# Seven products with features and rests side by side, output tiles kept in PSUM, and w_out's rests on GpSimd

## What is computed

```python
def swiglu(x, w_in, w_out):
    gate, up = jnp.split(x @ w_in, 2, axis=-1)
    return (jax.nn.silu(gate) * up) @ w_out
h = layer_norm(DN_ALPHA * h + 0.5 * swiglu(h, ffn_w_in[i, 0], ffn_w_out[i, 0]), ln_g[i, 0], ln_b[i, 0])
```

## Time and profile before

| | |
|---|---|
| median of three runs | 2694.2 us |
| profiled execution | 2693.18 us, span 2691.6 us |
| mean granted clock of TensorE | 0.997 |
| TensorE busy | 2646.5 us, 98%, 15,901 matmuls |
| VectorE busy | 1937.9 us, 72% |
| ScalarE busy | 1123.7 us, 42% |
| GpSimd busy | 577.0 us, 21% |
| memory | 99 GB/s over the span |

### The profile page before, as it was taken

The page is one execution under the profiler, slowest core; times in us unless marked ns, Lnnn a source line. Parts: engine busy times, 40 slices in busy tenths (PEclk is TensorE's granted clock), DMA queues, the critical chain, the costliest instruction groups (busy, mean ns, idle before and its releaser), DMA issues.

```text
span 2691.6 us, 38695 instructions
## 1 busy us (share of the span) xinstructions
PE 2646.5 (98%) x15901; PEld 2303.0 (86%) x15901; DVE 1937.9 (72%) x2651; ACT 1123.7 (42%) x1624; POOL 577.0 (21%) x366
## 2 busy tenths in 40 slices
PE   9899999999999999999999999999999999999998
PEld 6787877678899997888999988999988888889997
DVE  7888634656888865448888778888655745788876
ACT  4444555543433445353434444434432332444343
POOL 2211000101444400001544214444000000044440
PEclk9999999999999999999999999999999999999999
DMA  9543222212333332222333323333323223233331
GB/s 303 157 150 107 63 63 63 79 52 78 122 94 106 99 110 66 92 63 73 116 97 121 108 72 121 95 107 98 110 83 110 78 72 110 78 108 97 94 110 63
DMA packets 297891, 268.34 MB, mean 100 GB/s; under 512 B 11047, under 2 KB 265265, under 8 KB 297586
## 3 DMA queue, kind: packets, MB, share of 16 engines
q1 hardware_dynamic: 294050, 256.99, 30.9%
q0 software_dynamic: 2368, 6.64, 0.7%
q10 hardware_dynamic: 1296, 2.23, 0.3%
HBM read 263.72 MB, written 2.10 MB: 99 GB/s over the span
## 4 chain that ended last, share of the span: by engine, by line
PE 81%; DVE 12%; ACT 3%; issue 3%; POOL 1%; DMA 0%; DVEq 0%; POOLq 0%; ACTq 0%
PE psum L368 14%; PE psum L370 14%; PE psum L369 14%; PE psum L448 7%; PE psum L449 7%; PE psum L450 7%; PE psum L424 2%; PE psum L425 2%; PE psum L426 2%; PE psum L3040 1%; DVE w_lo L353 1%; DVE w_lo L1130 1%; PE psum L3053 1%; PE psum L1621 1%; PE psum L2608 1%
## 5 line engine op out<-in xcount | busy, mean ns | idle before, releaser
L368 PE MATMUL psum<-h_hi,w_hi 128*128 128x256 f32 (+1 forms) x2224 | 720.0, 324 | 12.8 <-DVE consts L1153 4.2
L370 PE MATMUL psum<-h_hi,w_lo 128*128 128x256 f32 (+1 forms) x2224 | 701.8, 316 | 0.0
L369 PE MATMUL psum<-h_lo,w_hi 128*128 128x256 f32 (+1 forms) x2224 | 701.4, 315 | 0.0
L368 PEld LDWEIGHTS psum<-h_hi,w_hi 128*128 128x128 f32 x2224 | 425.5, 191 | 47.7 <-issue 9.7
L369 PEld LDWEIGHTS psum<-h_lo,w_hi 128*128 128x128 f32 x2224 | 425.5, 191 | 28.4 <-issue 4.8
L370 PEld LDWEIGHTS psum<-h_hi,w_lo 128*128 128x128 f32 x2224 | 425.1, 191 | 27.0
L1076 POOL TENSOR_TENSOR val<-w_raw 128x512 f32<-128x512 f32 x72 | 100.4, 1395 | 963.5 <-DMA w_raw<-in_ffn_w_in 567.9
L353 DVE TENSOR_TENSOR w_lo<-w_raw,w_hi 128x2048 fp32r<-128x2048 f32 x98 | 223.1, 2287 | 83.4 <-ACT w_hi L348 77.3
L544 DVE SCALAR_TENSOR_TENSOR acc<-psum,acc 128x512 f32<-128x512 f32 x374 | 242.2, 679 | 36.0 <-PE psum L450 35.4
L368 PE MATMUL psum<-t_hiffn,w_hi 128*128 128x256 f32 x864 | 244.9, 283 | 0.4
L369 PE MATMUL psum<-t_loffn,w_hi 128*128 128x256 f32 x864 | 244.5, 283 | 0.0
(11 more groups left out here) (460 smaller groups left out, 5603.0 us busy)
## 6 DMA issues: line engine op xcount, KB each, us to landing
w_raw<-in_ffn_w_in SPq DMA_DIRECT2D x176, 512.0 KB, 5.0
w_raw<-in_ffn_w_out SPq DMA_DIRECT2D x88, 512.0 KB, 6.2
w_raw<-in_ret_w_in SPq DMA_DIRECT2D x48, 512.0 KB, 4.6
ada_raw<-in_ada_w SPq DMA_DIRECT2D x32, 512.0 KB, 4.4
w_raw<-in_odd_w_in SPq DMA_DIRECT2D x32, 512.0 KB, 4.8
w_raw<-in_even_w_in SPq DMA_DIRECT2D x24, 512.0 KB, 6.1
w_raw<-in_gla_w_in SPq DMA_DIRECT2D x24, 512.0 KB, 4.8
ada_first<-in_ada_w SPq DMA_DIRECT2D x32, 256.0 KB, 6.2
```

What stands on the lines that cost most here:

```text
L368: k.nc.tensor.matmul(out, ws, xs, start=first, stop=False)
L369: k.nc.tensor.matmul(out, ws, xl, start=False, stop=False)
L370: return k.nc.tensor.matmul(out, wl, xs, start=False, stop=last)
```

## The change

- The rounded features and their rests get neighbouring places in one tile (`k.h`, `k.t`). A group of three 256-column matmuls in the seven products becomes one of 512 columns (rounded weights by rounded features and rests, into the two halves of a bank) and one of 256 columns (`beside`). It concerns rounds 2 to 10 of the four stages.
- Each product then has two halves in its bank, and VectorE adds both (`add_product`, and the new lines of `vector_mid`). The second addition takes the first one's result and waits for it. Product 1 of the next half waits for f_u where it waited for f_p1.
- Of the output tiles of rounds 0 to 7 the four that are made last stay in their PSUM banks; the next round begins with the same tiles and accumulates on them (`kept`, `onto_kept`, `out_order`). VectorE adds only the other four to `acc`.
- The rests of w_out for rounds 2 to 8 are made by GpSimd (`gpsimd_rest`, one subtraction of 128x2048), in its queue between the sums of "a" and those of "b", instead of by VectorE's L353. TensorE and SP wait for GpSimd's event there (`rest_done`).

```diff
+def kept(r):
+    return r < ROUNDS - 3
+def out_order(n):
+    stage, what, r = PIECES[n]
+    return (4, 5, 6, 7, 0, 1, 2, 3) if stage[:3] == "ffn" and what == "o" and r < ROUNDS - 2 and r % 2 else tuple(range(8))
+def onto_kept(n, j):
+    stage, what, r = PIECES[n]
+    return stage[:3] == "ffn" and what == "o" and 0 < r < ROUNDS - 2 and kept(r - 1) and j in out_order(n)[:4]
...
+def pool_rest(n):
+    stage, what, r = PIECES[n]
+    return stage[:3] == "ffn" and what == "o" and SEVEN <= r < ROUNDS - 2
+def rest_done(n):
+    return ("pool_w" if pool_rest(n) else "w_lo", n)
+def gpsimd_rest(k, n):
+    k.nc.gpsimd.wait_ge(*k.at("w_hi", n))
+    k.nc.gpsimd.tensor_tensor(k.lo(n), k.w_raw[:, buffer(n), :], k.hi(n).bitcast(F32), SUB).then_inc(*k.up("pool_w", n))
 def sync_piece(k, n):
     if n in (SLOTS, SLOTS + 1):
         k.nc.sync.wait_ge(*k.at("used", n - SLOTS))
     elif n > SLOTS:
-        k.nc.sync.wait_ge(*k.at("w_lo", n - SLOTS))
+        k.nc.sync.wait_ge(*k.at(*rest_done(n - SLOTS)))
...
+def beside(k, bank, ws, wl, x, first, last):
+    k.nc.tensor.matmul(bank.rearrange("p (a n) -> p a n", a=2), ws, x, start=first, stop=False)
+    return k.nc.tensor.matmul(bank[:, 0:256], wl, x[:, 0, :], start=False, stop=last)
...
-    onto = seeded(n, j)
+    onto = seeded(n, j) or onto_kept(n, j)
...
-    pe.wait_ge(*k.at("w_lo", n))
+    pe.wait_ge(*k.at(*rest_done(n)))
     pe.wait_ge(*k.at(*ready[0]))
-    for j in range(4):
-        pe.wait_ge(*k.at(*free[j]))
+    tiles = out_order(n)
+    for j in tiles[:4]:
+        if not onto_kept(n, j):
+            pe.wait_ge(*k.at(*free[j % 4]))
         out_part(k, n, j, order[0], True, False, hi, lo)
     pe.wait_ge(*k.at(*ready[1]))
-    for j in range(8):
-        if j >= 4:
-            pe.wait_ge(*k.at("acc", (n, j - 4)))
+    for j in tiles:
+        if j not in tiles[:4]:
+            pe.wait_ge(*k.at("acc", (n, j ^ 4)))
             out_part(k, n, j, order[0], True, False, hi, lo)
         ins = out_part(k, n, j, order[1], False, True, hi, lo)
-        ins.then_inc(*(k.up("out", (n, j)) if j < 7 else k.up("used", n)))
+        ins.then_inc(*k.up(*out_done(n, j)))
...
-    return ("out", (n, j)) if j < 7 else ("used", n)
+    return ("out", (n, j)) if j != out_order(n)[-1] else ("used", n)
...
-            event = ("f_p1", "f_c11", "f_c12", "f_c21")[x]
+            event = ("f_u", "f_c11", "f_c12", "f_c21")[x]
...
-        (wh, wl), (xh, xl) = w_block(k, n, a), h_block(k, stage, b)
+        (wh, wl), both = w_block(k, n, a), h_beside(k, stage, b)
         for kk in range(4):
             w = slice(kk * P, (kk + 1) * P)
-            ins = three(k, k.bank[bank][:, 0:256], wh[:, w], wl[:, w], xh[:, kk, :], xl[:, kk, :],
-                        kk == 0, kk == 3)
+            ins = beside(k, k.bank[bank][:], wh[:, w], wl[:, w], both[:, :, kk, :], kk == 0, kk == 3)
...
+def add_product(k, b, out, onto):
+    ve = k.nc.vector
+    ve.tensor_tensor(out, onto, k.bank[b][:, HALF[0]], ADD).then_inc(*k.dve.up())
+    ve.wait_ge(*k.dve.at())
+    return ve.tensor_tensor(out, out, k.bank[b][:, HALF[1]], ADD)
 def vector_mid(k, stage, r, s, x):
     ve, key = k.nc.vector, (stage, r, s)
     u, c22, e, p1 = k.f_c[stage][:, 0, :], k.f_c[stage][:, 1, :], k.f_h[:, s, HALF[1]], k.f_h[:, s, HALF[0]]
-    ve.wait_ge(*k.at("f_p", key + (x + 1,)))
     if x == 0:
         ve.wait_ge(*k.at("f_p1", key))
-        ve.tensor_tensor(u, p1, k.bank[1][:, 0:256], ADD).then_inc(*k.up("f_u", key))
+        ve.tensor_tensor(p1, p1, k.bank[0][:, HALF[1]], ADD).then_inc(*k.dve.up())
+        ve.wait_ge(*k.at("f_p", key + (1,)))
+        ve.wait_ge(*k.dve.at())
+        add_product(k, 1, u, p1).then_inc(*k.up("f_u", key))
     elif x == 1:
+        ve.wait_ge(*k.at("f_p", key + (2,)))
         ve.wait_ge(*k.at("f_u", key))
-        ve.tensor_tensor(e, u, k.bank[2][:, 0:256], ADD).then_inc(*k.up("f_e", key))
+        add_product(k, 2, e, u).then_inc(*k.up("f_e", key))
     else:
+        ve.wait_ge(*k.at("f_p", key + (3,)))
         ve.wait_ge(*k.at("f_e", key))
-        ve.tensor_tensor(c22, e, k.bank[3][:, 0:256], ADD)
-        ve.tensor_tensor(u, u, k.bank[3][:, 0:256], ADD).then_inc(*k.up("f_g", key))
+        ve.tensor_tensor(c22, e, k.bank[3][:, HALF[0]], ADD)
+        ve.tensor_tensor(u, u, k.bank[3][:, HALF[0]], ADD).then_inc(*k.dve.up())
+        ve.wait_ge(*k.dve.at())
+        ve.tensor_tensor(c22, c22, k.bank[3][:, HALF[1]], ADD)
+        ve.tensor_tensor(u, u, k.bank[3][:, HALF[1]], ADD).then_inc(*k.up("f_g", key))
 def vector_c11(k, stage, r, s):
     ve, key, p1 = k.nc.vector, (stage, r, s), k.f_h[:, s, HALF[0]]
     ve.wait_ge(*k.at("f_p", key + (4,)))
-    ve.tensor_tensor(p1, p1, k.bank[1][:, 0:256], ADD).then_inc(*k.up("f_c11", key))
+    add_product(k, 1, p1, p1).then_inc(*k.up("f_c11", key))
 def vector_c12(k, stage, r, s):
     ve, key, e = k.nc.vector, (stage, r, s), k.f_h[:, s, HALF[1]]
     ve.wait_ge(*k.at("f_p", key + (5,)))
-    ve.tensor_tensor(e, e, k.bank[2][:, 0:256], ADD).then_inc(*k.up("f_c12", key))
+    add_product(k, 2, e, e).then_inc(*k.up("f_c12", key))
 def vector_products(k, stage, r, s):
     ve, key, c = k.nc.vector, (stage, r, s), k.f_c[stage]
     ve.wait_ge(*k.at("used", AT[stage, "ab"[s], r]))
     ve.wait_ge(*k.at("f_g", key))
-    ve.tensor_tensor(c[:, 0, :], c[:, 0, :], k.bank[3][:, 0:256], ADD).then_inc(*k.up("f_c21", key))
+    add_product(k, 3, c[:, 0, :], c[:, 0, :]).then_inc(*k.up("f_c21", key))
...
-        vector_piece(k, AT[stage, "o", r - 1])
+        if not pool_rest(AT[stage, "o", r - 1]):
+            vector_piece(k, AT[stage, "o", r - 1])
...
-            vector_outs_ffn(k, stage, r - 1, range(4, 6))
+            if not kept(r - 1):
+                vector_outs_ffn(k, stage, r - 1, range(4, 6))
             vector_unit_s(k, n, 1)
-            vector_outs_ffn(k, stage, r - 1, range(6, 8))
+            if not kept(r - 1):
+                vector_outs_ffn(k, stage, r - 1, range(6, 8))
...
 def vector_outs_ffn(k, stage, r, outs):
+    n = AT[stage, "o", r]
     for j in outs:
-        vector_out(k, AT[stage, "o", r], j, r == 0)
+        vector_out(k, n, out_order(n)[j], r < 2 and j < 4)
...
             gpsimd_sums(k, stage, r, s)
+            if s == 0 and r >= SEVEN + 2:
+                gpsimd_rest(k, AT[stage, "o", r - 2])
...
-    k.h_hi, k.h_lo = sb("h_hi", [P, KD, T], F32R), sb("h_lo", [P, KD, T], F32R)
+    k.h = sb("h", [P, 2, KD, T], F32R)
+    k.h_hi, k.h_lo = k.h[:, 0, :, :], k.h[:, 1, :, :]
...
-            k.t_hi[stage], k.t_lo[stage] = (sb(n + stage, [P, 3, 4, 256], F32R, c2) for n in ("t_hi", "t_lo"))
+            k.t[stage] = sb("t" + stage, [P, 2, 3, 4, 256], F32R, c2)
+            k.t_hi[stage], k.t_lo[stage] = k.t[stage][:, 0, :, :, :], k.t[stage][:, 1, :, :, :]
...
```

More of the change, by code:

```diff
@@ L929, in h_block, with h_beside @@
     return k.h_hi[:, 4 * half:4 * half + 4, HALF[c]], k.h_lo[:, 4 * half:4 * half + 4, HALF[c]]
+def h_beside(k, stage, x):
+    if x in T_BLOCK:
+        return k.t[stage][:, :, T_BLOCK[x], :, :]
+    half, c = H_BLOCK["B12" if x == "T1" else x]
+    return k.h[:, :, 4 * half:4 * half + 4, HALF[c]]
 def w_blocks(k, n, unit, count):
@@ L1337, in vector_seventh @@
     vector_unit_a22(k, n)
-    vector_outs_ffn(k, stage, r - 1, range(4, 8))
     vector_unit_s(k, n, 0)
@@ L1375, in vector_ffn @@
     vector_t_rest(k, stage, "T1")
-    vector_outs_ffn(k, stage, 0, range(4, 8))
     vector_seventh(k, stage)
@@ L3863, in tiles @@
     k.lng, k.lnb = sb("lng", [P, D]), sb("lnb", [P, D])
-    k.f_oh_hi, k.f_oh_lo, k.w4_hi, k.w4_lo, k.t_hi, k.t_lo, k.f_c = {}, {}, {}, {}, {}, {}, {}
+    k.f_oh_hi, k.f_oh_lo, k.w4_hi, k.w4_lo, k.t, k.t_hi, k.t_lo, k.f_c = {}, {}, {}, {}, {}, {}, {}, {}
     k.f_h = k.const("reset128", 0, 2 * T).rearrange("p (a n) -> p a n", n=T)
```

## The result

The changed kernel takes 2857.1 us (median of 4 runs, 2855.1 to 2858.4) against 2694.6 for the kernel before (2692.4 to 2696.4): 1.0603 times as long, 95% interval 1.059 to 1.0616, or 162.6 us more. The profiled execution took 2855.9, its span 2854.5.

What follows compares the result with a forecast made beforehand. The changed stage was taken as bound by TensorE, VectorE's queue close behind. Stalls of 2.0, 0.9 and 1.2 less 0.7 gained, 3.4 us a round x 28 = 95, plus 22 for rounds 2 and 10: +117, 2810 us; range 2728 to 2882.

Steps and rivals of the forecast that it cites:

- rival A: GpSimd's subtraction gets in ahead of L1140 (now L1188); TensorE stalls 3.2 us there, 5.7 a round, 2875 us; chance 0.16.
- order of forecast: In the "a" half, L1140 (now L1188) runs to 8.7 us, then GpSimd's subtraction from 8.6 to 13.2.
- the walk: VectorE's queue followed in written order through a middle round (3 to 9): 3.4 us more a round, 95 in all.
- the stalls: TensorE waits of 2.0 us for f_u and 0.9 for f_g in the "b" half, 1.2 at the output's fifth tile.
- TensorE's gain: One 512- and one 256-column matmul replace three of 256: 12.6 ns saved per group, 0 to 25.4 us, upper taken.
- VectorE's load: Seven adds of a half become fifteen, 7.8 us more a round; less removed work, net +3 on 25.3: fits as a sum.
- the block: VectorE instructions with both inputs in SBUF wait out GpSimd's 4.59 us subtraction; the "a" pair, ready at 11.35, waits until 13.2.
- The kept tiles give TensorE nothing: TensorE did not wait for evacuations before; the tiles' worth is only 2.4 us in VectorE's queue.
- Rounds 2 and 10: Rounds outside the walk: round 2 costs between 2 and 7 us, 4 taken; round 10 +1.6; 22 over four stages.
- rival B: GpSimd's subtraction falls into gaps of VectorE's two-input work: 1.4 us a round, +61, 2754 us; chance 0.20.
- C: VectorE keeps up, f_u of the "b" half being the place; only TensorE's term stands, 2668 us; 0.03 for it and stalls cancelling.
- Rival D: The 512-column matmul saves nothing: forecast with 25 us more, 2835; forecast and this together 0.47.

Runs made afterwards that it cites:

- kept alone: The kernel before with only the kept output tiles: no 512-column matmuls, w_out's rests on VectorE; 2698.7 us, ratio 1.0017.
- no second adds: The changed kernel without VectorE's additions of the second bank halves and with w_out's rests on VectorE; 2684.0 us, 0.996 times the kernel before.
- rests on VectorE: The changed kernel with w_out's rests made by VectorE again, nothing on GpSimd but its sums; 2796.8 us, 1.0375 times the kernel before.
- waits: The changed kernel with one more wait on GpSimd, so its subtraction starts only after VectorE's L1188; 2810.6 us, 1.0428 times the kernel before.

## Why the prediction was right and wrong

The time lay in the range and on the forecast side, 47 us above the forecast; the mechanism was rival A's (2875, given 0.16), 18 us above what was measured. The 162.6 us, split by the runs, each difference with one part changed:

```
kept tiles                        (kept alone - before)            +4.2
512-column matmuls                (no second adds - kept alone)   -14.7
second-half adds                  (rests on VectorE - no adds)   +112.8
subtraction on GpSimd, order of forecast  (waits - on VectorE)    +13.8
the same ahead of L1188           (changed - waits)               +46.6
```

- **The step that failed** is in the walk: "It ends near 7.5; L1140 waits for that, runs to 8.7". `gpsimd_sums` started at 1.73, not near 1.9, took 5.3 us, at 1.30 to 1.32 an instruction, and ended at 7.04; I had carried over 5.6 from a "b" piece, beside which VectorE's pair ran (803.00). With L1188 due at 7.3, as forecast (875.52 is 7.29), the subtraction was first. Two events "within 0.3 us" can't be put in order from sums of such rows. That deserved near even chances, not 0.47 against 0.16; a start 0.5 us later gave the forecast's order, in round 8 of ffn11.
- **Given the order, the walk holds.** The run with the wait is 2810.6 against the forecast's 2810. That it comes so close is partly luck: the stalls came out 0.4 us a round shorter than forecast and TensorE's gain 0.3 smaller, and the two cancel. Its stalls are 1.49, 0.51 and 0.82 as shown; a shown wait starts at a modelled end, and each costs 0.27 more than that between starts (0.16 of the last matmul's overlap and 0.1 of a longer first one), so 1.8, 0.8 and 1.1 against 2.0, 0.9 and 1.2. For the changed kernel the same count gives 4.61 + 4 x 0.27 - 0.38 = 5.3 a round, the 5.3 measured; rival A had 5.7.
- **VectorE's load** was the main term, and it was right that it fits as a sum and not where TensorE waits: 30.77 us busy in 36.37, some 4.2 of them L1188 held in the block. That is 85%, where the forecast named near 90% as its sign. Dependent adds are 0.44 to 0.46 apart inside `add_product` (871.24 to 871.70) and 0.51 to 0.54 across its events, where I took 0.51 for all.
- **TensorE's gain** was mis-sized: 6.8 ns a group, 13.7 us in all, not 12.6 and 25.4. Neither end of 0 to 12.6 was it; the middle would have been the better guess for an operand that no row showed. The Trainium skill ("TensorE: Matmul & The Clock Gate", Back-to-back issue gap) would have made it 5 us, an estimate; the measured 14 lies between.
- **The block** is as told: the trace agrees with the Trainium skill ("SBUF - State Buffer", Who interferes with whom) in the rows shown, 5.40 us at L1188, 2.84 and 4.81 for the pair and for one of its two, and 0.42 for adds with an operand in PSUM.
- **"The kept tiles give TensorE nothing"** was right in steady rounds, and missed that four evacuations less in round 2 move two-input work into GpSimd's way: +4.
- **Rounds 2 and 10** were right: round 2 cost 3.75 us a stage where I took 4, and all outside rounds 2 to 9 5.4 us, 1.35 a stage, where I took 1.6 for round 10. The steps in them were not separated by a run.
- **Round 3** is not the middle round of the walk: its L1188 goes first, and it cost 4.1 us, less than the 5.3 of rounds 4 to 9.
- **The range's lower end**, 2728, is 26 us under rival B, where the bounds given for round 2 make 8. It played no part.
- Rivals B and C are out: in none of the 28 rounds were L1188 and the pair of "a" both free of the block, and VectorE did not keep up even without GpSimd's part (2796.8). Rival D was partly so, by half the gain.

## What to carry to other kernels

Before work is moved from VectorE to GpSimd, lay both engines' two-input instructions on one time axis: what counts is which VectorE instructions fall inside the moved one, since each is held until it ends, and a long one that wins by a quarter of a microsecond cost VectorE 4.2 of its 4.6 us here, and the kernel 2.0 us a round. A product that TensorE makes in fewer instructions but leaves in more pieces is paid by the engine that collects them: here 14 us were won and 113 paid. Where two events are nearer to each other than the rows' error, give both orders about equal chances.

## What the runs showed that I had not expected

TensorE's granted clock fell in the changed kernel. Two stretches of the trace (the clock is the third from last column), and TensorE's timeline right after a wait for L1188:

```profile
796.00:804.00 8.00, 8.00 (x47) 6.96 (x46) 4.80 (x10) 2.93 (x3) 6.62 (x5) 1.00 0.04 11
804.00:812.00 8.00, 5.25 (x22) 4.27 (x21) 7.18 (x9) 1.48 (x4) 3.09 (x1) 0.79 0.34 99
```

```profile
808.22 0.74 PE L408 MATMUL psum<-h,w_hi 128*128 128x512 f32 x1 [2.75 <-DVE w_lo L1188]
808.76 0.41 PE L409 MATMUL psum<-h,w_lo 128*128 128x256 f32 x1
808.98 0.63 PE L408 MATMUL psum<-h,w_hi 128*128 128x512 f32 x1
```

After standing for 2.75 us TensorE ran at the lower level, 1.2 GHz, for 3.4 us: a 256-column matmul starts 0.22 before the next one, not 0.12. The run has 24 stretches at that level, 95.4 us in all, against 4 with 20.0 before. Of the 24, 15 begin at a wait for L1188, and 6 at a wait for f_u (L1196) of 1.9 to 3.4 us in round 2 or 3. Not every such wait brings one: the clock stayed at the upper level after 8 of the 23 waits for L1188, the 2.71 us one shown above among them. In time they cost nothing that shows: the steady round with a mean clock of 0.95 (832.11 to 868.49) and the one at 1.00 (868.49 to 904.86) are 36.38 and 36.37 us long. In the slower one TensorE waits only for L1188 and L585; the two waits for L1196 and L1220, 0.54 and 0.48, are gone. VectorE sets the pace there, and the slow stretch fills what would have been waiting.

In pairs a matmul's distance to the next is not that of its own width in the earlier trace rows. A 512-column start is 236 ns ahead of the 256-column one, and that 117.5 ahead of the next 512, against 227 and 120 there. With four of a width together the 512 are at 232.5 and the 256 still at 117.5, so the alternation is only a part of the difference.
